# Expert rows by selection products from the residual, and a router without column groups, in a decoder step on one core

## The reference

```python
h = rms_norm(x, norm_ffn).reshape(B * L, D)
g_logits = jnp.einsum('nd,dg->ng', h, router_group_w) + router_group_b
g_idx = jnp.argmax(g_logits, axis=-1)
e_logits = jnp.einsum('nd,dge->nge', h, router_expert_w) + router_expert_b   # the row's group is taken
top_w, top_i = lax.top_k(jax.nn.softmax(e_logits, axis=-1), 2)
gate = jnp.einsum('nd,edf->nef', h, w_gate)        # e: 16, d: 1024, f: 512
up = jnp.einsum('nd,edf->nef', h, w_up)
act = jax.nn.silu(gate) * up * combine[..., None]
x = x + jnp.einsum('nef,efd->nd', act, w_down)
```

## Time and profile before

| | |
|---|---|
| runs, us | 818.65, 819.46, 820.51; median 819.46 |
| profiled execution, us | 820.81 |
| its span, us | 819.0 |
| mean granted TensorE clock | 0.947 of full |
| busy in the span: TensorE, VectorE, ScalarE, GpSimd | 90%, 47%, 27%, 7% |
| moved by DMA | 172.98 MB, mean 211 GB/s |
| chain that ended last: TensorE, VectorE, DMA, ScalarE, issue | 55%, 9%, 4%, 4%, 5% |

### The profile page before, as it was taken

How to read it: one execution, slowest core, us unless ns; L and a number is a source line. 1 busy time by engine, 2 the same in 40 slices (tenths; PEclk the granted TensorE clock), 3 DMA queues, 4 the chain that set the end, 5 groups by cost and what they waited for, 6 DMA issues and landing times.

```text
span 819.0 us, 12490 instructions
## 1 busy us (share of the span) xinstructions
PE 737.8 (90%) x4713; PEld 397.8 (49%) x4713; DVE 381.7 (47%) x884; ACT 218.6 (27%) x561; POOL 56.7 (7%) x87
## 2 busy tenths in 40 slices
PE   4985899979999888989979977689999999999987
PEld 2454346434654543545545644345555545454532
DVE  5421102476230567787876865366144332423146
ACT  1211111111220455657756831001110101010113
POOL 0111000120000000000000000110000000000040
PEclk9999699998999769999989998689999999999999
DMA  9135880638523970000000157689899999999992
GB/s 327 33 93 166 235 314 2 231 115 223 176 102 122 269 307 0 2 3 1 1 27 1 64 156 270 198 278 323 278 400 406 405 407 399 408 401 401 408 387 107
DMA packets 99423, 172.98 MB, mean 211 GB/s; under 512 B 21314, under 2 KB 38562, under 8 KB 99330
## 3 DMA queue, kind: packets, MB, share of 16 engines
q1 hardware_dynamic: 87986, 150.76, 52.2%
q10 hardware_dynamic: 8112, 11.24, 3.7%
q0 software_dynamic: 3264, 10.17, 3.5%
HBM read 152.95 MB, written 21.28 MB: 213 GB/s over the span
## 4 chain that ended last, share of the span: by engine, by line
PE 55%; DVE 9%; issue 5%; DMA 4%; ACT 4%; ACTq 0%; POOL 0%; DVEq 0%; SPq 0%
PE bank L2392 18%; PE bank L2825 6%; PE bank L1797 5%; PE bank L2383 4%; PE bank L2807 4%; PE bank L2426 4%; PE bank L1724 3%; PE bank L1743 3%; PE bank L2516 1%; PE bank L2511 1%; DMA work<-h_rows,ids 1%; DVE st L1372 1%; ACT work L2682 1%; PE bank L2375 1%; PE bank L2439 1%
## 5 line engine op out<-in xcount | busy, mean ns | idle before, releaser
L2825 PE MATMUL bank<-reg 128*128 128x512 f32 (+1 forms) x384 | 167.8, 584 | 1.2 <-DVE reg L2766 0.9
L2392 PE MATMUL bank<-reg,qreg 128*32 128x128 f32 (+2 forms) x848 | 130.5, 389 | 0.8 <-issue 0.8
L2825 PEld LDWEIGHTS bank<-reg 128*128 128x128 f32 x384 | 72.5, 198 | 70.8 <-issue 68.1
L2392 PEld LDWEIGHTS bank<-reg,qreg 128*32 128x32 f32 (+2 forms) x848 | 66.8, 139 | 59.6 <-issue 48.3
L2807 PE MATMUL bank<-cf,reg 128*128 128x128 f32 (+1 forms) x384 | 63.9, 287 | 27.0 <-ACT work L2682 9.7
L1797 PE MATMUL bank<-reg 128*128 128x512 f32 x128 | 66.1, 641 | 0.4 <-DVE x L1504 0.3
L2807 PEld LDWEIGHTS bank<-cf,reg 128*128 128x128 f32 (+1 forms) x384 | 43.6, 146 | 45.0 <-issue 34.9
L2682 ACT ACTIVATE work<-bank 128x128 f32<-128x128 f32 (+6 forms) x107 | 40.9, 413 | 45.3 <-PE bank L2807 44.6
L2766 DVE COPY work<-bank 128x128 f32<-128x128 f32 (+4 forms) x56 | 23.3, 429 | 55.5 <-PE bank L2807 55.4
L1212 ACT ACTIVATE reg<-bank,st 128x128 f32<-128x128 f32 (+3 forms) x64 | 33.2, 525 | 35.6 <-DVE st L1372 35.4
L1743 PE MATMUL bank<-work,vreg 128*64 128x128 f32 x480 | 39.0, 294 | 2.4 <-DVE work L2766 2.4
(11 more groups left out here) (338 smaller groups left out, 927.6 us busy)
## 6 DMA issues: line engine op xcount, KB each, us to landing
reg<-w_gate SPq DMA_DIRECT2D x12, 2048.0 KB, 20.3
reg<-w_up SPq DMA_DIRECT2D x12, 2048.0 KB, 22.7
reg<-w_down SPq DMA_DIRECT2D x12, 2048.0 KB, 20.6
reg<-w_in SPq DMA_DIRECT2D x16, 512.0 KB, 6.1
expert_rows<-vreg SPq DMA_DIRECT2D x11, 512.0 KB, 5.4
reg<-cache_sb_k SPq DMA_DIRECT2D x16, 256.0 KB, 4.7
reg<-cache_sb_v SPq DMA_DIRECT2D x16, 256.0 KB, 3.8
qreg<-w_up SPq DMA_DIRECT2D x2, 2048.0 KB, 16.6
```

The source lines that it names most:

```text
L2392: ins = T.matmul(bank[which][rows, at_:at_ + w], rowsT[b][:, k, r0:r0 + n], w_[:, k, h * w:(h + 1) * w], start=(k == 0), stop=(k == KD - 1))
L2825: ins = nc.tensor.matmul(at("m", ("proj", n))[:, 0:w], hT[:, k, i * P:(i + 1) * P], win[:, pos % 2, k, 0:w], start=(k == 0), stop=(k == KD ...
```

## The change

- **Router.** `parts` and its copy are gone. `group` makes the 20 logits of a row in eight products with the transposed rows as the stationary side, added up in one bank. For the last tile logits and rank are in ring `x`, else in `t`.
- **Expert 0's rows.** `rowsT` is made on TensorE: for each block of 128 features and each tile, x (stationary) times a mask of 0 or the row scale, with a one-hot column for each of the 128 rows of the block (`first_rows[0]`, made by `make_rows`). Seven feature blocks accumulate over the five tiles in seven bank parts, tile by tile; the eighth (k = 7) is done for all tiles at the end. ScalarE and VectorE copy out with the norm's gain (`first_out`). `ids0`, `first_ids`, the gather and its transposes are gone.
- **Expert 1's rows.** The same with masks of 96 columns, all 40 products after expert 0's up product, in place of gather and transposes.
- **Order.** h2 of the last tile is made after the count of the experts; `sort_experts` stands in the middle of expert 0's gate product, `sort_ids` after its up product.
- **Queues.** SP waits before load 6 for logits and order, and for the stored h2 only before load 7. POOL's read of the table waits for h2 too; gathers begin with expert 2, two at once.
- `extra`, scratch of VectorE, gets memory of its own; it was in `gain`, which h2 still reads.

```diff
+    first_rows = [view(work, 5120, [TILES, P]), view(work, 6144, [TILES, SIZES[1]])]
...
         if n == 4:
             mix_scales(QT - 1)
-        if n == 5:
-            route_parts(QT - 2)
+        if n in (6, 10, 11):
+            make_rows(tile_order[(6, 10, 11).index(n)])
         if n == 8:
             route_group(QT - 2)
             route_choice(QT - 2)
         if n == 12:
             rank(QT - 2)
+            make_rows(QT - 2)
+            rank_slots(QT - 2)
+            rank_exps(QT - 2)
     for half in range(2):
         transpose_ffn(QT - 1, half)
-    rest_of_rows(QT - 1)
-    route_parts(QT - 1)
+    ffn_squares(QT - 1)
+    ffn_scale(QT - 1)
+    for k in range(4):
+        use("m", ("first", k), "act")
+    use("o", ("first", 4), "dve")
+    for k in (5, 6):
+        use("t", ("first", k), "dve")
+    step("first", QT)
     route_group(QT - 1)
     route_choice(QT - 1)
+    for i in range(QT - 1):
+        step("first", i)
     rank(QT - 1)
-    route_weights(QT - 2)
-    route_weights(QT - 1)
+    make_rows(QT - 1)
+    use("o", ("first", 7), "dve")
+    step("first", QT - 1)
+    rank_slots(QT - 1)
+    step("first_out")
+    rank_exps(QT - 1)
...
+        elif kind == "first_out":
+            for k in range(4):
+                sg.wait(act, "m_full", ("first", k))
+                nc.scalar.activation(rowsT[0][:, k, :], first_part(k), ACT.Copy, scale=gainR[:, k:k + 1]
+                                     ).then_inc(sg["m_act"], 1)
...
+        elif kind == "make_rows":
+            i, = key
+            r = ROWS[i]
+            if i == QT:
+                sg.wait(dve, "square_sums", QT - 1)
+            if i != QT - 1:
+                second_rows(i, r)
+            V.tensor_scalar(first_rows[0][0:r, i, :], c["count"][0:r, 0:P], rows_col(i, 2), rows_col(i, 0),
+                            ALU.is_equal, ALU.mult).then_inc(sg["rows0"], 1)
...
-        elif kind == "parts":
...
-            for half in range(2):
-                for q in range(4):
-                    ins = T.matmul(at("t", ("parts", i))[32 * q:32 * q + 32, 0:r], wr[:, 4 * half + q, :],
-                                   h2T[:, 4 * half + q, 0:r], start=(half == 0), stop=(half == 1))
-            ins.then_inc(sg["t_full"], 1)
         elif kind == "group":
             i, = key
             r = ROWS[i]
-            acquire(pe, "t", ("logit", i))
-            sg.wait(pe, "t_act", ("parts", i))
-            T.matmul(at("t", ("logit", i))[0:r, 0:20], parts[:, 0:r], c["fold"], start=True, stop=True
-                     ).then_inc(sg["t_full"], 1)
...
+            acquire(pe, route_ring(i), ("logit", i))
+            for half in range(2):
+                wait_transposed(pe, ("h2T", i, half))
+                for k in range(4 * half, 4 * half + 4):
+                    ins = T.matmul(at(route_ring(i), ("logit", i))[0:r, 0:20], h2T[:, k, 0:r], wr[:, k, 0:20],
+                                   start=(k == 0), stop=(k == KD - 1))
+            ins.then_inc(sg[route_ring(i) + "_full"], 1)
+        elif kind == "first":
+            i, = key
+            r, n = ROWS[i], tile_order.index(i)
+            sg.wait(pe, wout_ring(i) + "_dve", ("wout", i, last_group(i)))
+            sg.wait(pe, "rows0", i)
+            for k in (4, 5, 6, 0, 1, 2, 3):
+                if n == 0:
+                    acquire(pe, first_ring(k), ("first", k))
+                ins = T.matmul(first_part(k), x[0:r, i, k * P:(k + 1) * P], first_rows[0][0:r, i, :],
+                               start=(n == 0), stop=(n == TILES - 1))
+                if n == TILES - 1:
+                    ins.then_inc(sg[first_ring(k) + "_full"], 1)
...
+    ffn_rows(QT - 1)
+    route_weights(QT - 2)
+    route_weights(QT - 1)
     use("x", ("order",), "dve")
     use("x", ("idx",), "dve")
     step("ids_row")
...
         elif kind == "experts":
-            sg.wait(sp, "t_full", ("logit", QT - 1))
-            sp.wait_ge(sg["st_h2"], sg.total["st_h2"])
-            sp.wait_ge(sg["e_x0"], 16)
+            sg.wait(sp, "x_full", ("logit", QT - 1))
             sg.wait(sp, "x_dve", ("order",))
...
+                if n == RING - 1:
+                    sp.wait_ge(sg["st_h2"], sg.total["st_h2"])
...
+                if j == 1:
+                    sg.wait(pe, "r_max", QT - 1)
+                    for half in range(2):
+                        for k in range(4):
+                            for t, i in enumerate(tile_order):
+                                ins = T.matmul(bank[3 + half][:, k * n:(k + 1) * n],
+                                               x[0:ROWS[i], i, (4 * half + k) * P:(4 * half + k + 1) * P],
+                                               first_rows[1][0:ROWS[i], i, :], start=(t == 0), stop=(t == TILES - 1))
+                        ins.then_inc(sg["e_rowsT_full"], 1)
+                    return
...
             acquire_all(pe)
-            sort_experts()
-            rows_of(0)
             for j in range(NE):
...
-                gate_or_up(j, 0, sg["e_gate"])
-                if j == 0:
-                    sort_ids()
+                gate_or_up(j, 0, sg["e_gate"], sort_experts if j == 0 else None)
...
                 gate_or_up(j, 1, sg["e_up"])
+                if j == 0:
+                    sort_ids()
```

More of the change, by code:

```diff
@@ L651, in rank, with make_rows, rank_slots @@
     def rank(i):
-        use("t", ("rank", i), "dve")
+        use(route_ring(i), ("rank", i), "dve")
         step("rank", i)
+    def make_rows(i):
+        step("make_rows", i)
         sg.mark("rows0", i)
-        if i == QT - 1:
-            use("x", ("ids0",), "dve")
-            step("ids0")
-            sg.mark("ids0", 0)
+    def rank_slots(i):
         step("slots", i)
@@ L792, in place_output, with rows_col, second_rows, route_ring @@
             place(now + SHARE * group + 28, add_product, i, group)
+    def rows_col(i, n, width=1):
+        return rt[0:ROWS[i], 84 + 4 * i + n:84 + 4 * i + n + width]
+    def second_rows(i, r):
+        nc.vector.tensor_scalar(first_rows[1][0:r, i, :], c["count"][0:r, 0:SIZES[1]], rows_col(i, 3), rows_col(i, 1),
+                                ALU.is_equal, ALU.mult)
+    def route_ring(i):
+        return "x" if i == QT - 1 else "t"
+    def first_ring(k):
+        return "m" if k < 4 else "t" if k in (5, 6) else "o"
+    def first_part(k):
+        return at(first_ring(k), ("first", k))[:, P * (k // 7):P * (k // 7) + P]
     def place_route(i, first):
@@ L798, in place_route @@
         place(now - 41, transpose_ffn, i, 1)
-        place(now + 57, route_parts, i)
         place(now + 86, ffn_squares, i)
@@ L804, in place_route @@
         place(now + 270, ffn_rows, i)
-        place(now + 305, rank, i)
+        for f in (rank, rank_slots, rank_exps):
+            place(now + 305, f, i)
         place(now + 340, route_weights, i)
@@ L1296, in route_choice @@
                         ).then_inc(sg["onehot"], 1)
-        V.tensor_tensor(rt[0:r, 82:83], chosen[0:r, i, 0, 0:1], chosen[0:r, i, 1, 0:1], ALU.add)
+        sg.wait(nc.vector, "onehot", i)
+        V.tensor_scalar(rows_col(i, 0, 2), onehot[0:r, i, 0:2], small[0:r, 12:13], None, ALU.mult)
     def dve_more(dve, link, kind, key):
@@ L2037, in expert_gps @@
             sg.wait(pool, "x_dve", ("idx",))
[L2038 to L2040 removed]
+            pool.wait_ge(sg["st_h2"], sg.total["st_h2"])
+            for j in range(2, NE):
+                if j >= 4:
+                    pool.wait_ge(sg["e_rowsT_full"], 2 * (j - 2))
                 nc.gpsimd.indirect_dma_start(rows_in[j % 2][0:SIZES[j]], None, h2_dram,
@@ L2384, in product, with gate_or_up @@
                 return ins
-            def gate_or_up(j, which, sem):
+            def gate_or_up(j, which, sem, between=None):
                 b, w_ = j % 2, chunk(("gate", "up")[which], j)
@@ L2390, in gate_or_up @@
                     for k in range(KD):
+                        if between and k == KD // 2:
+                            between()
                         for rows, h in column_groups(n):
```

130 lines of the change are left out of this document (55 added, 75 removed).

## The result

The changed kernel takes 831.33 us (median of 828.31, 830.59, 832.06 and 834.78), the kernel before, run beside it, 819.06: ratio 1.0163, 95% interval 1.0102 to 1.0223. A repetition gave 1.019 (1.0152 to 1.0228). By the medians it is slower by 12.3 us, in the repetition by 16.6. I forecast 821.9 and a range of 816.8 to 826.0: the sign was right, the size far too small, and the range does not hold the time.

What follows compares the result with a forecast made beforehand. TensorE's time through experts 0 and 1 was taken to bound the end, with the weight loads following it. Attention +3.2 and later stages -0.8 gave +2.4 us on the 819.46 median: 821.9 us, range 816.8 to 826.0.

Steps and rivals of the forecast that it cites:

- So both stand behind the time at which TensorE gets through experts 0 and 1.: Weight loads and TensorE's later work both follow experts 0 and 1; moving expert 1's gate product moves the end as much.
- Item 1: Router in the attention, tiles 0, 1 and sample tile: ungrouped products cost more, a mask leaves; +3.2 us, bounds -0.3 to +4.3.
- A delay in the attention does the same: A delay in the attention moves the kernel's end by as much.
- Rival (a): Attention: the router's extra products hide in TensorE's 11.1 us waits for ScalarE; 818.4 us, or 817.0 with cheaper rows; chance 0.36.
- Item 2: Tile 2's router and masks beside the last output product: TensorE is full there, so the last addition ends 0.9 us later.
- Item 3: Last tile, from transposes through logits, rank and expert 0's selected rows: its gate product starts at 521.6 us, was 521.97.
- rival (b): Last tile: the clock falls between 507 and 511 us and halves the pace of following products; 824.9 us, chance 0.15.
- Item 4, expert 1's rows: Selecting expert 1's rows on TensorE, 40 products: 64 rows at 0.11 and 16 at 0.09 us, 8.5 us in all.
- Item 4, the gate product of expert 1: It starts at 545.5 us (was 544.28) but takes 5.56 at full clock, not 7.61, so ends 0.8 us earlier.
- Rival (c): Selection rows of experts 0 and 1: float32 load and stream do not overlap; +10.9 us, 832.8 us, chance 0.05.
- Rival (d): Experts' row selection: the gather is gone but selection replaces it as a wait; already half of the sum, no separate chance.
- Queues: SP's seventh load starts near 527 us, the table lands before the ids product, later gathers leave near 537; cover suffices.

Runs made afterwards that it cites:

- the router's own run: Kernel before with only the router changed: eight products one after another, no column groups, parts copy or fold; 817.76 us, ratio 0.9992.
- its pads: Kernel before with unused bytes added on chip: 128 bytes 823.23 us, 64 bytes 823.63, 256 bytes 818.29, three pads aligning all eight weight buffers 817.32.

## Why the prediction was wrong, point by point

- **"So both stand behind the time at which TensorE gets through experts 0 and 1."** The half on TensorE holds: 9.3 us less there brought the time down by about 8 to 12. The step that failed is the silent one beside it, that the loads "from there follow each other" at an unchanged 5.6 us each. They came at (770.26 - 580.45)/33 = 5.75 us, because the buffers had moved. This term, missing from my sum, is worth 0.52% (4.3 us) in the kernel before, and about 5 us in the changed one: the ratios 1.0163 and 1.019 against 1.013 and 1.0102 put it between 3 and 7. The narrower constants stood in the whole diff.
- **Item 1, attention +3.2.** Right as a price, as far as the traces show. Tile 0 and tile 1 each add the forecast 1.5 us on the spot (1.56 and 1.57); sixteen ungrouped rows at 0.112 are 1.8 us, between my 1.70 and the 2.1 that I set beside it. From tile 0's addition to the fourth from the last it is 101.1 us before and 104.4 in the change's repetition, with as much time at half clock: +3.3. The first profile of the change has 101.4 there, since its clock fell for 6.8 us less. Rival (a), the attention hides the router, had 0.36; its cause did not happen, though by the router's own run the time moved by less than the 4.1 us of items 1 and 2. "A delay in the attention does the same" is thus not shown for the router: 1.4 us came back in the last tile, where I had expected at most 0.1.
- **Item 2, +0.9.** Right: the last four additions span 12.94 us instead of 12.10 (509.01 - 496.07 against 505.48 - 493.38). VectorE's masks did not hold them up.
- **Item 3, expert 0's gate product.** I had 15.2 us after the start of the last addition (506.4 to 521.6), it is 18.9. "With TensorE busy the clock should stay at 1.00" fails one step earlier: rival (b), chance 0.15, is what happened. The clock is at half level for 6.8 us while TensorE is full, which costs 3.4 us of work at full clock. I priced it at 3.0. The row price of 0.128 was too high; 0.112 for the 42 + 14 rows gives back 0.9. Along the stage, 0.9 of the 3.7 us arise up to the end of the logits, 2.1 in the 42 rows and the rank, 0.8 from tile 3's products on. Clock and row price make 2.5 of them; the other 1.2 are not traced to a single term, but column block 7, which changes the height too, takes 1.5 us to the next start where I had 1.2.
- **Item 4, expert 1's rows.** 8.5 us forecast, 11.64 measured; the wide rows were right (0.11 for 0.112). The step that failed is "16 at 0.09": the 8-row products start 112 ns apart among themselves, and each pair of them between 128-row ones costs 0.33 us more for the two changes of height. The 0.107 that I set beside my price is near the 0.112, and leaves the changes out as mine did. This is the mis-sized term, +3.1. A sign of it stood in the trace of before: its 32-row transposes start 62 ns apart, but the next product after them comes after 150.
- **Item 4, the gate product of expert 1.** It takes 5.56 us, as forecast. But the credit for it, 7.61 - 5.56 = 2.05 us, was a gain over one execution: of the seven profiles with the old experts (before, its repetition, its pads, the router alone), four show the clock fall there and three, the repetition among them, have 5.56 too. Of the seven profiles of changed kernels none shows it. The seven old ones have 6.7 us in the mean, so the credit is real, at about half its size.
- **Rival (c), load and stream not overlapping at 0.213.** Wrong in cause (0.213 is the price of the lower clock), though the time that it gave, 832.8, is near.
- **Rival (d), the selection takes the gather's place as a wait.** True for expert 0: from the start of the last addition to the end of its gate product it is 521.97 + 10.10 - 505.48 = 26.6 us before and 533.60 + 3.70 - 510.91 = 26.4 in the run with the gather of expert 1.
- **Queues.** SP's load 6 at 525.78 (forecast 527), the table read at 523.64, gathers at 535.95, with no wait of TensorE for them: right.

The sum, anew: +2.4 as forecast, +1 for the half of the clock's credit that belonged to one execution, +3.7 in item 3, +2.9 between the gate products (26.8 against 23.9), about +5 for the stream: +15, against +12.3 and +16.6 measured.

## What to carry to other kernels

When a diff changes the size of anything that is laid out ahead of DMA destinations, work out where they come to lie, and keep the large ones at multiples of 256 bytes; a stream that bounds the kernel feels it. Price a TensorE row by rows of its kind and by the neighbours it has: a product of few rows between full ones costs more than a full one. And before a gain is credited to a clock that comes back, look at a second trace for the same fall; when two traces are compared over a stretch, compare the time at half clock in it first, or a real cost of 4 us can look as if it had been given back.

## What the runs showed of the hardware

- From 600 to 700 us the stream ran at 401 to 404 GB/s with six of eight buffers at multiples of 256 bytes on chip and at 390 to 392 with them 64 or 128 bytes off; gathered rows of 4096 bytes took 187 to 188 ns instead of 173. The two buffers at 96 and 224 bytes past a multiple in the kernel before cost little in the mean over all packets of 2048 bytes (85.7 against 85.2 ns when they were moved too), but they cost: 15% of these packets took over 84 ns before, 4% with all eight at multiples, 73% with 128 bytes of pad, which leaves none at one. It is not every load: counted off by bytes, the load into `qreg` near 666 us has a mean of 88.5 ns before and 84.0 when moved, the one into `vreg` ahead of it 84.0 in both.
- Float32 product rows with 128 stationary columns started 112 ns apart at 2.4 GHz, for 20, 96 and 128 moving columns, and 213 to 214 at 1.2 GHz, seen for 20 and 128.
- An 8-row product between 128-row ones lengthened the four distances around it from 447 to about 780 ns; 8-row products that followed each other started 112 ns apart.
- In the last tile the clock fell in every profile: for 17 us in the seven with the old experts, much of it spent waiting, for 6.8 us in the seven changed ones. TensorE was busy for 9.1 to 9.8 of the 17 us, and for all of the 6.8.
- In the attention 3.4 us at half clock made the same stretch between two additions about 1.5 us longer: 16.5, 18.0 and 19.4 us with none, 3.4 and 6.8 us of it.
